# Weight roundings moved into two norms and out of the last step of an output, and feed-forward parts begun with three results at once instead of four

## What is computed

```python
def _layer(x, ...):
    h = _rmsnorm(x, norm_g)
    p = _split_columns(h @ w_in)
    ...
    merge = jax.nn.sigmoid(p['merge'].reshape(B, S, N_BRANCH, D_MODEL))
    merged = jnp.sum(merge * jnp.einsum('bsnc,ncd->bsnd', ys, w_branch), axis=2)
    return x + merged @ w_out
```

```python
def _conv_ffn(h, w_in, conv_w, conv_b, w_out):
    g, val = jnp.split(h @ w_in, 2, axis=-1)
    return (jax.nn.gelu(_dwconv(g, conv_w, conv_b), approximate=True) * val) @ w_out
...
        xl = xl + mod_l[5] * _conv_ffn(_modulate(xl, mod_l[3], mod_l[4]), ...)
        if not last:
            xc = xc + mod_c[5] * _conv_ffn(_modulate(xc, mod_c[3], mod_c[4]), ...)
```

## Time and profile before

| | |
|---|---|
| median of 3 runs | 3820.01 us (3816.85 to 3829.04) |
| the profiled execution's own time | 3820.42 us |
| its span in the trace | 3819.1 us |
| mean granted clock of TensorE | 0.95 of 2.4 GHz |
| busy: PE, DVE, ACT, POOL | 3431.2, 1720.4, 1276.9, 920.8 us |

### The profile page before, as it was taken

The page is one execution under the profiler, slowest core; times in us unless marked ns, Lnnn a source line. Parts: engine busy times, 40 slices in busy tenths (PEclk is TensorE's granted clock), DMA queues, the critical chain, the costliest instruction groups (busy, mean ns, idle before and its releaser), DMA issues. The chain is left out here.

```text
span 3819.1 us, 44449 instructions
## 1 busy us (share of the span) xinstructions
PE 3431.2 (90%) x17216; PEld 2679.8 (70%) x17216; DVE 1720.4 (45%) x3160; ACT 1276.9 (33%) x2188; POOL 920.8 (24%) x395
## 2 busy tenths in 40 slices
PE   5988998999889898899986888899999898888999
PEld 3765777777666677677675556788888656667877
DVE  3228333534234732543489554522264565544234
ACT  2322323333332232433321432322243345543322
POOL 2212121124312212112322202222364100023443
PEclk9999898999999898999988898999999899999999
DMA  3332112123343202213211101112242110012222
GB/s 140 144 149 81 34 62 75 53 84 113 133 154 126 73 32 72 67 55 113 91 50 45 50 1 45 46 60 67 67 135 92 49 57 1 1 56 75 97 96 81
DMA packets 87619, 288.48 MB, mean 76 GB/s; under 512 B 9968, under 2 KB 20592, under 8 KB 86512
## 3 DMA queue, kind: packets, MB, share of 16 engines
q1 hardware_dynamic: 86400, 275.80, 21.0%
q10 hardware_dynamic: 1008, 9.83, 0.7%
HBM read 281.40 MB, written 4.19 MB: 75 GB/s over the span
## 5 line engine op out<-in xcount | busy, mean ns | idle before, releaser
L394 POOL TENSOR_TENSOR weights_low<-weights_loaded,weights_high 128x1024 fp32r<-128x1024 f32 (+2 forms) x378 | 907.1, 2400 | 2881.5 <-ACT weights_high L376 2835.0
L307 PE MATMUL psum<-h_high,weights_high 128*128 128x512 f32 (+1 forms) x2400 | 925.2, 385 | 74.7 <-DVE h_low L554 24.9
L308 PE MATMUL psum<-h_low,weights_high 128*128 128x512 f32 (+1 forms) x2400 | 896.2, 373 | 0.0
L309 PE MATMUL psum<-h_high,weights_low 128*128 128x512 f32 (+1 forms) x2400 | 894.8, 373 | 0.0
L307 PEld LDWEIGHTS psum<-h_high,weights_high 128*128 128x128 f32 x2400 | 464.5, 194 | 172.0 <-issue 77.6
L376 ACT CAST weights_high<-weights_loaded 128x1024 fp32r<-128x1024 f32 (+2 forms) x378 | 392.2, 1037 | 515.3 <-PE psum L309 482.2
L308 PEld LDWEIGHTS psum<-h_low,weights_high 128*128 128x128 f32 x2400 | 464.7, 194 | 83.7 <-issue 10.0
L309 PEld LDWEIGHTS psum<-h_high,weights_low 128*128 128x128 f32 x2400 | 463.0, 193 | 79.2
L3520 DVE TENSOR_TENSOR act_low<-ffn_act,act_high 128x512 fp32r<-128x512 f32 (+1 forms) x66 | 143.7, 2177 | 143.1 <-ACT act_high L3490 143.0
L307 PE MATMUL psum<-act_high,weights_high 128*128 128x512 f32 (+1 forms) x528 | 189.5, 359 | 11.1 <-DVE act_low L3520 6.2
L308 PE MATMUL psum<-act_low,weights_high 128*128 128x512 f32 (+1 forms) x528 | 189.0, 358 | 0.0
(11 more groups left out here) (436 smaller groups left out, 5080.6 us busy)
## 6 DMA issues: line engine op xcount, KB each, us to landing
weights_loaded<-stream_dram SPq DMA_DIRECT2D x478, 512.0 KB, 3.3
weights_loaded<-stream_dram SPq DMA_DIRECT2D x80, 128.0 KB, 3.2
weights_loaded<-stream_dram SPq DMA_DIRECT2D x16, 384.0 KB, 3.1
weights_loaded<-stream_dram SPq DMA_DIRECT2D x8, 272.0 KB, 2.7
x<-x_dram SPq DMA_DIRECT2D x1, 2048.0 KB, 8.9
arena_mem<-mem_dram ACTq DMA_DIRECT2D x2, 1024.0 KB, 6.5
x<-x_dram ACTq DMA_DIRECT2D x1, 2048.0 KB, 8.0
x_kept_dram<-x ACTq DMA_DIRECT2D x1, 2048.0 KB, 7.7
```

The source lines that it names most:

```text
L307: pe.matmul(out, a.high, b.high, start=start, stop=False)
L308: pe.matmul(out, a.high, b.low, start=False, stop=False)
L309: return pe.matmul(out, a.low, b.high, start=False, stop=stop)
L394: pool.tensor_tensor(self.low[s][:, 0:size], raw[:, 0:size], self.high[s][:, 0:size], ALU.subtract).then_inc(*g.event("weights_low").up(po ...
```

## The change

Four things. The norms of the first block's two layers get `rounds`, the four chunks of the first group of gates, so that ACT casts them between the high parts of h (with the usual two chunks ahead, three at the first call). The group of a feed-forward part has three results (gate 0, value 0, gate 1, chunks of 768 columns), and value 1 follows as a result of its own with a chunk of 1024; one more call of `round` stands behind the gelu of f = 1. In the output the rounding at the last f of a side stops one chunk short (`min(2, 22 - f)` is 1 at f = 21). And in layer 0 the squares of the context side stand ahead of the rounding of step 22 instead of behind it and behind the high part of step 24, and DVE makes the context's residuals after the low part of step 22 instead of step 23.

```diff
@@ -2070,7 +2070,7 @@
         if not n.added:
             squares_scalar(g, n, [])
         root_scalar(g, n)
-        apply_scalar(g, n)
+        apply_scalar(g, n, rounds=[("z_part", l, 0, part) for part in range(KT // Z_PER)])
         fill_scalar(g)
         if l:
             act.dma_start(g.dram.x_kept, g.t.x[:, :, :]).then_inc(*S("x_kept").up(act, 0, 16))
@@ -3348,9 +3348,10 @@
 def ffn_in_tensor(g, l, norms, spans, turn):
     t = g.t
     each = modulated(g, norms)
-    project_group(g, ("ffn_first", l), [("ffn_gate", l, 0), ("ffn_value", l, 0), ("ffn_gate", l, 1), ("ffn_value", l, 1)],
-                  turn, np.concatenate([np.arange(P), FFN + np.arange(P), P + np.arange(P), FFN + P + np.arange(P)]),
-                  "ffn_w_in_2", (l,), t.ffn[l].h2, spans, each)
+    project_group(g, ("ffn_first", l), [("ffn_gate", l, 0), ("ffn_value", l, 0), ("ffn_gate", l, 1)], turn,
+                  np.concatenate([np.arange(P), FFN + np.arange(P), P + np.arange(P)]), "ffn_w_in_2", (l,),
+                  t.ffn[l].h2, spans, each)
+    project_wide(g, ("ffn_value", l, 1), turn, FFN + P + np.arange(P), "ffn_w_in_2", (l,), t.ffn[l].h2, spans, each)
     for f in range(2, FT):
@@ -3385,7 +3386,7 @@
-        if f > 1:
+        if f > 0:
             g.weights.round(("ffn_value", l, f))
@@ -3499,11 +3500,11 @@
     if with_ctx:
         act.preload_act_table_set("natural_log_exp_and_others")
     for s, (side, lo, n, f) in enumerate(steps):
-        g.weights.round(("ffn_out_w", l, side, f))
+        if with_ctx and s == FT:
+            squares(1)
+        g.weights.round(("ffn_out_w", l, side, f), min(AHEAD, FT - 1 - f + NSPLIT - TAIL))
         if s + 2 < len(steps):
             high(*steps[s + 2])
-        if with_ctx and s == FT:
-            squares(1)
     if with_ctx:
         squares(0)
 
@@ -3534,7 +3535,7 @@
     for s, step in enumerate(steps):
         low(*step)
-        if with_ctx and s == FT + 1:
+        if with_ctx and s == FT:
             residuals(1, CTX)
     residuals(0, SEQ)
```

## The result

The changed kernel took 3784.5 us in the median of 4 runs (3775.7 to 3791.6), against 3820.2 of the kernel before on the same chip: a ratio of 0.9905, 95% interval 0.9879 to 0.9931. That is 35.7 us; the forecast was 3786 and 34.0. The profiled execution took 3791.6 us (span 3790.3), so it alone shows only 28.8 us. I therefore compare stretches: each runs from the start of a matmul ahead of an edit to the start of one behind it, and both are found by counting, so that the same matmuls lie between them in every kernel.

The account below looks back on a forecast made before the run. PE, busy nine tenths of the span, was taken as the bound, with idle stretches and half-clock matmuls to remove. Terms 14.0 + 5.9 + 3.2 + 3.6 + 7.3 = 34.0 us gave 3786 us, range 3775 to 3801.

Parts of the forecast that it names:

- Part 1: First block's two norms: casting gate chunks inside the norm starts the gates earlier, 14.0 us gained, from 0 to 14.
- the copies of the adaLN rows and the DMA that keeps x slip: First block's norms: these slip some 15 us behind the casts, but nobody reads them until the branches; nothing charged.
- Part 2: Feed-forward beginnings: three results at once remove PE's wait for bank 2, gaining 5.9 us in layer 0, 3.2 in layer 1.
- the new wait: Layer 1's feed-forward: PE waits 2.1 us at value 2, whose chunk is cast behind the second gelu.
- the 1.4 for the clock: A 1.4 us charge for slower matmuls after PE's idle, at layer 1's value 2 and one step into the latent side.
- Part 3, middle: First output, between context and latent side: earlier residuals gain 5.0 less 1.4 us for the clock, 3.6, from 0 to 6.
- Part 3, end: End of first output: adds run beside PE, sums start 8.7 us earlier, 1.4 paid back; 7.3 taken, 5 to 9.5.
- All else is PE work without holes: Outside the listed idle stretches PE works without holes, so time won at the edits should reach the end.
- 1 (roundings bring nothing): First block's norms: casts hold up high parts, so moving them gains nothing; 3800 us, chance 0.12.
- 2 (starving): Feed-forward groups: three results at once starve PE, idling some 2.3 us a part with clock falling; 3834 us, chance 0.04.
- 3: First block's norms and last norm: POOL holds the port through its subtracts, delaying DVE; 3791 us, chance 0.10.
- 4 (no clock cost behind the shorter idles): Behind the shorter idles the clock costs nothing and the norm keeps up; 3780 us, chance 0.09.

Follow-up runs that it names:

- e10: Changed kernel with one call of round fewer in the first block's norms, so the sixth cast stands behind the adaLN copies again: 3782.0 us, ratio 0.9894.
- second profile: Profile from a further run of the changed kernel, unchanged: median 3785.3 us, ratio 0.9893 to the kernel before.
- e1: Kernel before with only the gate chunks cast inside the first block's two norms: 3811.2 us, ratio 0.9975.
- e3: Kernel before with only the first output's step between the sides changed (short rounding on the context side, squares and residuals earlier): 3816.7 us, ratio 0.9988.
- e6: Changed kernel with value 2's chunk cast right behind gate 0's copy instead of behind the second gelu: 3785.8 us, ratio 0.9904.
- e8: Changed kernel with two results at once in the feed-forward groups, gate 1 and value 1 as results of their own: 3803.1 us, ratio 0.9940.
- e2: Kernel before with only the feed-forward group of three results, value 1 behind it and one more rounding: 3809.7 us, ratio 0.9970.
- e12: Changed kernel with one call of round fewer in the first block's norms, run once more: 3780.8 us, ratio 0.9900.

## Why the prediction was right

- **Part 1, 14.0 forecast.** 12.4 and 11.1 in the two profiles, 10.8 and 9.1 (trace and median) alone. The idle times shrank by 6.6 and 8.0, as worked out. The failed term is a zero: "the copies of the adaLN rows and the DMA that keeps x slip" was held free since nobody reads them early. But the tanh stands behind the copies on ACT, and gives PE its banks. Price 2.0; e10 removes it. In the second profile and in e1 the adaLN matmuls themselves also took 1.0 and 1.2 us longer than before in the two layers together; over all profiles they take 15.1 to 17.9, so I don't put this down to the change. The forecast also counted eight casts moved, four a layer; there are six a layer, since each call casts ahead.
- **Part 2, 5.9 and 3.2 forecast.** 5.0 and 4.9. In layer 0 I charged nothing for h_low: the first 144 matmuls took 28.2 us in all eight profiles of kernels with three at once, where they took 27.2 before. Seven of them show a wait of 0.62 on h_low. The eighth, the first of after, shows none, but its first 24 matmuls had taken 0.7 us longer at the lower clock, and it came out the same: here DVE, not PE, sets the end. In layer 1 the new wait came (1.74 for 2.1), but not the 1.4 for the clock. Not foreseen: 1.6 at the second output's entrance.
- **Part 3, middle, 3.6 forecast.** 4.9: the idle time moved as said, and the 1.4 for the clock did not fall due in either profile of after. That is luck as far as this case shows: behind the same 2.20 us e3, e6 and e8 paid 1.6.
- **Part 3, end, 7.3 forecast.** 7.7: 8.65 less 1.0, for 8.7 less 1.4.
- **Sum.** 34.0 forecast, 34.8 at the six places and 36.4 with the entrances, 35.7 by the medians. Misses of −1.6, −0.9, +1.7, +1.3 and +0.4 nearly cancel; the total is nearer than its terms, by luck. "All else is PE work without holes" was not so (PE stands up to 22 us at a time between 1900 and 2320), but the change reached the end all the same.
- **Rivals.** 1 (roundings bring nothing) fell with e1. 2 (starving) is a real mechanism: at three results it costs 0.9 and 0.8 us in the two groups, of which 0.6 each is idle time, and at two the beginnings are another 7.2 and 4.4 longer. 3 fell by the norm's timeline. By the Trainium skill, SBUF — State Buffer, "Who interferes with whom", the first to issue holds the port for its whole instruction; the rows agree for single instructions (2.24 us instead of 0.69), and in the two rows of subtracts, of the first norm and of MLA's, DVE's waiting operation was the next to issue each time. The same section says that a DVE instruction with at most one SBUF input, outside the two-port modes, does not contend; the two taps beside the subtract in e6 agree (1.55 us with it and without). 4 (no clock cost behind the shorter idles) came true for both idles in after, though not for the reason that they are short: e3's 2.21 us were followed by a mean clock of 0.68, and e8's 2.06 by 0.60.

## What to carry over

Follow what stands behind a moved step on its own engine up to the next one that PE needs, even if the steps between are free: here two small copies cost 1 us a layer through the tanh behind them. Between two stages with a norm in the first, look at DVE's busy share of the stretch for the width chosen: at three results, where it is 96%, PE loses 0.9 us, and with two the norm sets the pace throughout. Judge gains of one or two microseconds by count over the same matmuls, up to the next idle time behind, since that is where the clock may take them back.

## What the runs showed that I had not expected

- An idle time of 2.70 us at the second output's entrance was followed by full clock in after (twice), e2, e10 and e12, and by a fall worth 1.4 to 1.6 us in all nine other profiles. Those five are the ones that begin with three results at once and cast value 2's chunk at its place in after. Each kernel that was profiled twice did the same both times, wherever the stretch stood in time. Between the sides, 2.20 us were followed by full clock in after (twice), e10 and e12, and by a fall in e3, e6 and e8. At the first output's entrance after did both (7.10 and 5.61 us in the table). What decides it stays open.
- Two executions of one kernel differed by 4.5 us over the same 86 matmuls (13.73 at 1.00, 18.23 at a mean clock of 0.75) with no idle time inside, and stood up to 12.9 us apart on the way, to end 2.7 apart.
